# Eight matmul units of the last query step placed in other rounds of a sparse attention, and half of its compressed attention one pass later

## What is computed

```python
qg = h @ w_qg                                   # queries and gates
q = qg[..., :1024] * 64 ** -0.5
# compressed: 15 pooled keys and values for each group
s = q @ k_cmp - slope * distance
p_cmp = softmax(where(vis, s, -1e30)) * vis
o_cmp = p_cmp @ v_cmp
# selected and sliding window, each over all 256 tokens here
o_slc = softmax(q @ k_slc - slope * dist, causal) @ v_slc
o_win = softmax(q @ k_win - slope * dist, causal) @ v_win
o = gate0 * o_cmp + gate1 * o_slc + gate2 * o_win
h = h + o @ w_o
```

## Time and profile before

| | us |
|---|---|
| median of 3 runs | 971.28 |
| lowest, highest | 971.02, 973.37 |
| the profiled execution | 971.64 |
| its span, first to last instruction | 969.6 |
| PE busy in it | 953.9 (98%) |
| DVE busy | 709.0 (73%) |
| ACT busy | 488.4 (50%) |
| POOL busy | 86.9 (9%) |
| DMA read | 185.09 MB, 192 GB/s over the span |

### The profile page before, as it was taken

One profiled execution on the slowest core, in us unless ns is written; L12 is line 12 of the kernel. 1 busy time (PEld: TensorE's weight loads), 2 busy tenths in 40 slices (PEclk: granted clock), 3 DMA queues, 4 the chain that ended last, 5 costly groups with the idle time before them and its releaser, 6 DMA issues.

```text
span 969.6 us, 19370 instructions
## 1 busy us (share of the span) xinstructions
PE 953.9 (98%) x7874; PEld 920.2 (95%) x7874; DVE 709.0 (73%) x1124; ACT 488.4 (50%) x712; POOL 86.9 (9%) x132
## 2 busy tenths in 40 slices
PE   8999999999999999899999999999999999999998
PEld 8999999999999977599999999999999999999998
DVE  4986777777769878967777777688876676555654
ACT  5444634444437556847344443537667555334441
POOL 7000000000000042420100000020000000000000
PEclk9999999999999999999999999999999999999999
DMA  9856848786754762037586868435344357564621
GB/s 262 273 174 215 261 156 293 230 292 224 271 184 150 249 218 88 1 133 259 166 303 224 294 228 288 145 114 181 101 171 153 109 174 260 171 221 132 229 72 44
DMA packets 131387, 186.98 MB, mean 193 GB/s; under 512 B 6272, under 2 KB 102656, under 8 KB 131328
## 3 DMA queue, kind: packets, MB, share of 16 engines
q1 hardware_dynamic: 123984, 159.82, 50.1%
q0 software_dynamic: 6912, 25.17, 7.5%
q10 hardware_dynamic: 432, 1.16, 0.4%
HBM read 185.09 MB, written 1.05 MB: 192 GB/s over the span
## 4 chain that ended last, share of the span: by engine, by line
PE 90%; DVE 5%; ACT 2%; issue 1%; DMA 1%; POOL 0%; SPq 0%; DVEq 0%; ACTq 0%
PE ps L1886 47%; PE ps L1962 19%; PE ps L1882 12%; PE ps L1884 4%; DMA g_raw<-in_a_w_in 1%; DVE g_lo L1172 1%; PE ps L2028 1%; PE ps L2146 1%; PE ps L2161 1%; DVE e_even L1535 1%; PE ps L2081 0%; POOL bias_h L629 0%; ACT e_odd L881 0%; PE ps L2270 0%; PE ps L1944 0%
## 5 line engine op out<-in xcount | busy, mean ns | idle before, releaser
L1886 PE MATMUL ps<-opa_hi,g_hi 128*128 128x256 f32 x864 | 228.9, 286 | 1.8 <-issue 1.4
L1886 PE MATMUL ps<-opa_lo,g_hi 128*128 128x256 f32 x864 | 221.0, 283 | 0.0
L1886 PE MATMUL ps<-opa_hi,g_lo 128*128 128x256 f32 x864 | 181.5, 283 | 0.0
L1288 DVE TENSOR_TENSOR g_lo<-g_raw,g_hi 128x2048 fp32r<-128x2048 f32 x54 | 123.8, 2293 | 69.7 <-ACT g_hi L742 69.7
L1886 PEld LDWEIGHTS ps<-opa_hi,g_hi 128*128 128x128 f32 x864 | 165.7, 192 | 5.1 <-issue 4.7
L1886 PEld LDWEIGHTS ps<-opa_lo,g_hi 128*128 128x128 f32 x864 | 162.7, 192 | 0.1
L1962 PE MATMUL ps<-hid_hi,d_hi 128*128 128x256 f32 x528 | 148.0, 280 | 0.1
L1172 DVE TENSOR_TENSOR g_lo<-g_raw,g_hi 128x2048 fp32r<-128x2048 f32 x54 | 123.5, 2289 | 33.4 <-ACT g_hi L668 32.9
L1962 PE MATMUL ps<-hid_hi,d_lo 128*128 128x256 f32 x528 | 147.7, 280 | 0.0
L1962 PE MATMUL ps<-hid_lo,d_hi 128*128 128x256 f32 x528 | 147.5, 279 | 0.0
L668 ACT ACTIVATE g_hi<-g_raw 128x2048 fp32r<-128x2048 f32 x54 | 103.1, 1910 | 71.8 <-PE ps L1886 55.2
(11 more groups left out here) (337 smaller groups left out, 1809.8 us busy)
## 6 DMA issues: line engine op xcount, KB each, us to landing
g_raw<-in_f_w_gu SPq DMA_DIRECT2D x44, 1024.0 KB, 8.8
ada_raw<-in_w_ada POOLq DMA_DIRECT2D x48, 512.0 KB, 6.1
d_raw<-in_f_w_down SPq DMA_DIRECT2D x22, 1024.0 KB, 5.1
g_raw<-in_w_in SPq DMA_DIRECT2D x14, 1024.0 KB, 7.9
g_raw<-in_w_gate SPq DMA_DIRECT2D x11, 1024.0 KB, 7.2
g_raw<-in_w_up SPq DMA_DIRECT2D x11, 1024.0 KB, 9.6
d_raw<-in_w_down SPq DMA_DIRECT2D x11, 1024.0 KB, 5.2
g_raw<-in_a_w_in SPq DMA_DIRECT2D x10, 1024.0 KB, 8.2
```

Of the source, the lines that this page charges most:

```text
L1288: dve.tensor_tensor(part_view(g_lo, g0 + r, True), raw_cols(c % 2, r % 2, True), part_view(g_hi, g0 + r, True).bitcast(F32), ALU.subtract) ...
L1886: mm = pe.matmul(pair(b)[:, a, :], wt[:, a * P:(a + 1) * P], xt, **st)
```

## The change

On PE, `values(0)` moves ahead of unit 8, and the eight units of step QG + 3 go two to each of blocks 2, 3, 4 and 5, where before there were four in block 2 and four in block 3. In block 5 both stand straight behind `scores(5)`. The wait for `evac_q(3)` and `compressed_scores(1)` move from block 4 to block 5, between `turn(4, 0)` and `turn(4, 1)`. In block 6 `turn(5, 0)` goes ahead of `values(4)`. On DVE, `evac_q(3)` moves from pass 4 to pass 5, ahead of `shift(10)`, and `compressed_shift(1)` from the end of pass 4 to right behind `shift(10)`. On ACT, `compressed_exp(1)` moves from the start of pass 5 to behind its three copies, and the split of WO + 1 from the end of pass 3 to the end of pass 6. The diff is whole.

```diff
--- before.py
+++ after.py
@@ -897,8 +897,6 @@
                 act.activation(pct[:, q, :], ps[:, 6 if q else 7, 0:T], ACT.Copy).then_inc(pct_made, 1)
 
             for j in range(1, NH // 2 + 2):
-                if j == 5:
-                    compressed_exp(1)
                 if 1 < j < NH // 2:
                     exps(j, 0)
                 if j >= 2:
@@ -910,8 +908,8 @@
                         if q == 0 and j >= 2:
                             act.wait_ge(pv_done, 2 * j - 2)
                         act.activation(pt_buf[:, 512 * q:512 * q + 512], ps[:, 4 + q % 2, :], ACT.Copy).then_inc(pt_copied, 1)
-                if j == 1:
-                    compressed_exp(0)
+                if j in (1, 5):
+                    compressed_exp(j // 5)
                 if j < NH // 2:
                     exps(j, 1)
                 if j == 1:
@@ -920,7 +918,7 @@
                     split_g(WO)
                 if j == 5:
                     compressed_copy(1)
-                if j == 3:
+                if j == 6:
                     split_g(WO + 1)
             product_and_gained(WO, 3, opb_hi, opb_hi_made, "f_norm", 8)
         if last_stage >= 4:
@@ -1576,10 +1574,12 @@
                 for e in range(2):
                     if j < NH // 2 + 1:
                         normalize(2 * j - 2 + e)
-                    if j == 4 and e == 0:
+                    if j == 5 and e == 0:
                         evac_q(3)
                     if j < NH // 2:
                         shift(2 * j + e)
+                    if j == 5 and e == 0:
+                        compressed_shift(1)
                 if j == 5:
                     compressed_factors(1)
                 dve.wait_ge(opa_hi_made, 8 * A_FILL["attn"] + j - 1)
@@ -1587,8 +1587,6 @@
                                   opa_hi[:, j - 2, :].bitcast(F32), ALU.subtract).then_inc(opa_made, 1)
                 if j == 3:
                     split_g(WO)
-                if j == 4:
-                    compressed_shift(1)
                 if j == 8:
                     split_g(WO + 1)
             add_product(WO, opb_hi, opb_lo, opb_hi_made, B_FILL["n3"], opb_made, "f_norm", 8)
@@ -2184,42 +2182,46 @@
 
             scores(2)
             compressed_turn(0)
+            values(0)
             query_units(8, 1)
-            values(0)
+            turn(1, 0)
             query_units(9, 1)
-            turn(1, 0)
+            turn(1, 1)
+
+            scores(3)
             query_units(10, 1)
-            turn(1, 1)
+            values(1)
+            turn(2, 0)
             query_units(11, 1)
-
-            scores(3)
-            query_units(12, 2)
-            values(1)
-            query_units(14, 1)
-            turn(2, 0)
-            query_units(15, 1)
             turn(2, 1)
 
             pe.wait_ge(g_evac, evacs(QG + 2))
             scores(4)
             values(2)
+            query_units(12, 1)
             turn(3, 0)
+            query_units(13, 1)
+            turn(3, 1)
+
+            scores(5)
+            query_units(14, 2)
+            values(3)
+            turn(4, 0)
             pe.wait_ge(g_evac, evacs(QG + 3))
             compressed_scores(1)
-            turn(3, 1)
-
-            scores(5)
-            values(3)
-            turn(4, 0)
             turn(4, 1)
 
             for j in (5, 6):
                 scores(j + 1)
                 if j == 5:
                     compressed_turn(1)
-                values(j - 1)
-                turn(j, 0)
-                turn(j, 1)
+                    turn(j, 0)
+                    values(j - 1)
+                    turn(j, 1)
+                else:
+                    values(j - 1)
+                    turn(j, 0)
+                    turn(j, 1)
 
             out_units(0, 0, 2)
             values(6)
```

## The result

The changed kernel takes 982.89 us in the median (982.09 to 983.68, 4 runs), the kernel before 972.1 in the same comparison (971.02 to 973.37). The ratio is 1.0109, 95% interval 1.0097 to 1.0121: slower by 1.1%, 10.8 us between the two medians. The forecast was slower by 6.6 us, with a range up to 980.0. The direction is right, the size is not. The profiled execution is the shortest of the four (982.09).

What follows compares the result with a forecast made beforehand. The prediction took a ring through PE, DVE and ACT, with DVE fullest, as the bound. Moved work (-2.1), new waits and work on DVE (net 5.2) and the split (1.4) gave +6.6 us: median 977.9, range 974.8 to 980.0.

Steps and rivals of the forecast that it cites:

- the ring: Attention passes, scores(2) to first output unit: a dependency cycle through PE, DVE and ACT, 6.0 us a round; loss +6.6 us.
- All three rivals with less or no loss: Same stretch: PE's holes filled, 968.0, chance 0.04; waits hidden, 970.1, 0.10; waits or split partly hidden, 974.2 to 976.3, 0.06.
- The first of them: PE as bound: four units (3.2 us) fill its 3.98 us of idle time, less a 0.7 wait; 968.0, chance 0.04.
- the term for the clock: Behind PE's 3.1 us gap ahead of turn(4,1): clock falls to 1.2 GHz, +0.4 to +1.1 us, 978.7, chance 0.07.
- the rule: Skill statement that long PE gaps lower the clock, weighed for the 3.1 us gap: 978.7, against 977.9 by the row.
- the cover of 0.3 us: Block 6: values(4) ends at 410.9, opa_hi not before 411.16, so putting turn(5,0) first was priced at 0.
- the turned order: Block 6, turn(5,0) ahead of values(4): price 0 with cover, at most the 1.89 us of values(4) without.
- the walk: Scheduling PE, DVE and ACT by row durations through blocks 2 to 6: first output unit at 419.88 instead of 413.28.
- the sum's terms: Blocks 4 to 6: -2.1 + 2.0 + 0.72 + 2.6 + 1.25 + 0.8 is 5.3 (unrounded 5.2), plus 1.4 for the split.
- the first two terms: DVE in pass 5: 2.0 us waiting for units 14 and 15, and 0.72 for evac_q(3), both added to the loss.

Runs made afterwards that it cites:

- a2: Changed kernel with 28 unread matmuls between compressed_scores(1) and turn(4,1) only, more than that gap holds; 984.61 us, ratio 1.0123 to the kernel before.
- a3: Changed kernel with ACT's split of WO + 1 at the end of its pass 4 instead of pass 6; 979.55 us, ratio 1.0065 to the kernel before.
- a4: Changed kernel with compressed_shift(1) behind shift(11) instead of behind shift(10); 978.14 us, ratio 1.0055 to the kernel before.
- The covers: Unread matmuls put into PE's gaps in the changed kernel; with 26 of them sized to the gaps of blocks 5 and 6 and ahead of turn(6,1), 978.56 us.
- a5: Changed kernel with evac_q(3) behind shift(10) instead of ahead of it; 981.14 us, ratio 1.0099 to the kernel before.
- a8: Changed kernel with the eight units back in blocks 2 and 3 and values(0) back behind unit 8; 976.82 us, ratio 1.0050 to the kernel before.
- a6: Changed kernel with values(4) ahead of turn(5,0) again, as before the change; 980.56 us, ratio 1.0077 to the kernel before.
- b2: Changed kernel with unread matmuls in the gaps of block 6 and ahead of turn(6,1), none ahead of turn(4,1); 979.89 us, ratio 1.0085 to the kernel before.
- a1: Changed kernel with 28 unread matmuls ahead of turn(4,1), more than that gap holds, and 18 between turn(6,0) and turn(6,1); 985.06 us, ratio 1.0130.
- b1: Changed kernel with only 11 unread matmuls in the gap ahead of turn(4,1); 980.75 us, ratio 1.0094 to the kernel before.
- a7: Changed kernel with 26 unread matmuls: 11 ahead of turn(4,1), 3 ahead of compressed_turn(1), 5 ahead of turn(5,0), 7 ahead of turn(6,1); 978.56 us, ratio 1.0071.
- b3: Changed kernel with compressed_shift(1) behind shift(11), ACT's WO + 1 split in pass 4, unread matmuls in block 6 and ahead of turn(6,1); 974.17 us, ratio 1.0021.

## Why the prediction was right and wrong

**Right: the ring, wait by wait.** With the clock held, the loss is 6.44 us where 6.6 were walked. In the changed kernel itself: evac_q(3) waits 1.9 (2.0 forecast) and begins at 395.99 us (395.8), compressed_shift(1) waits 2.5 (2.6) and begins at 400.38 (400.2), turn(4,1) begins at 403.14 (403.1) behind a gap of 2.8 (3.1), exps(7,0) follows the split without idle time. Only the gap ahead of turn(5,0) is 0.84 where over 1 was forecast. The wait for `pct` in block 2 is 0.5 (0.7), and scores(3) comes 0.9 us sooner without any gain, as argued. All three rivals with less or no loss were wrong for the reason given: DVE was there first. (The first of them had a slip: 3.2 us of units can return at most 3.2, not 3.98, which makes it 968.8 and not 968.0. Nothing hangs on it.)

**Wrong: the term for the clock, in size and in chance.** The step that failed is the weighing of the rule. The prediction saw a gap that no row of before matched, priced a fall of the clock at +0.4 to +1.1 us, and gave it 0.07. It cost 3.75 in the profiled execution; the other three are longer and have a lower mean granted clock (0.991 and 0.992, against 0.993). Three things were missed. (1) The length: only turn(4,1), scores(6) and turn(5,0) were doubled, as if the clock came back with the work; it stayed low for 10 us, which took in values(4), whose end moved past ACT's arrival, so that the cover of 0.3 us named for the turned order was gone and `opa_hi` waited 1.5. The whole stretch cost 2.2 where at most 1.1 was priced. (2) The second gap: the walk itself had ACT's first copy late behind the split and PE's last transposes waiting for it until 419.46, but the clock was not asked about there; the clock fell there too, and now in the output units, where PE has no idle time to give: 3.4 us at half rate cost 1.5, close to half of them, while the 10.2 us of the first stretch cost only 2.2. (3) The chance: the rows showed no fall up to a wait of 0.84 us and nothing about 3.1, so they gave no ground for 0.93 against a fall. The traces of a2 and a3 show that even the row was weak: there the clock fell ahead of scores(2) at waits of 0.65 and less, the same that stand in the kernel before. The statement of the Trainium skill ("TensorE: Matmul & The Clock Gate", section "HAM oscillation — how this bites in real kernels"), that long gaps of PE put the clock back, agrees with the trace: 2.8 us without work, then a granted clock of 0.50. Much shorter gaps went with a fall as well (1.2 and 1.3 us in a4), which this statement doesn't cover, and there the measurement decides. With the rule taken at its word, but the price taken as before, the forecast would have been 978.7, still 4 us short; with the price that the runs show, 6.6 + 3.75 is 10.35 us, where 10.8 were measured. The other statement of the Trainium skill that was weighed ("Perfetto Trace Analysis", section "Optimization Strategies"), to keep PE as busy as possible, did not make the moved units a gain. The covers, which are work for nobody, did gain by keeping PE busy, since what counted was the clock behind a gap.

**Partly wrong: the sum's terms.** The prediction listed on DVE 2.0 for the units, 0.72 for evac_q and 2.6 for the compressed scores as things that add. a5 shows that the first two are the shadow of PE's chain: taking 1.5 us out of the wait for the units put 1.3 into the next wait. The total was right, since both lists end at the same point, but someone who had taken the first two terms for something to win would have won nothing on the ring. Moving compressed_shift(1) and the split, with the gaps covered, returns 49.15 - 45.10 = 4.05 of the 6.4; by a8 the units are 1.4. The units were moved back only with the clock free to fall, so their 1.4 is read from the start of compressed_shift(1), ahead of the fall, and the exact share of each in the 6.4 stays open.

## What to carry to other kernels

Ask of every new gap on PE not only who waits for what, but what runs behind it: a price for a gap is the gap plus what the work behind it loses at half rate until the clock is back, as far as others wait for that work, and it is dearest where PE is the bound. Where an operation is moved to the middle of another engine's pass, walk the ring of all engines once around; the idle time of an engine that isn't the ring's slowest member is no room to fill. And when a wait looks like a term, look whether the next wait on the same engine would only grow by it.

## What the runs showed of the hardware

Each trace is one execution, so what follows counts cases and is not a rule. The gap of 2.8 or 2.9 us ahead of turn(4,1) was followed by a low clock in all six traces that left it uncovered (changed, a3, a5, a6, a8, b2), for 10.2 us in three of them, 6.8 in a5 and a8, and 3.4 in b2. With that gap covered or gone, two gaps of block 6 with two transposes between them (1.2 and 1.3 us in a1, a2 and a4; 0.87 and 1.27 in b1) had a fall in or behind them in all four, for 3.4 us. In a7 and b3, where no gap of blocks 5 and 6 was over 0.63 us, it didn't fall. The gap of 2.1 ahead of the last transposes was followed by a fall in the changed kernel, a4 and a6, and by none in a5 and a8.

Shorter gaps aren't safe either. Ahead of scores(2) every kernel has waits of about 0.4 to 0.65 us in the same order of work; the clock fell there in a2 and a3 and in none of the other eleven traces. The kernel before is no exception. It ran 28 more times beside the variants: the eleven executions with a mean granted clock of 0.999 or 1.000 took 971.2 to 972.3 us, the seventeen with 0.997 or 0.998 took 972.0 to 973.9; where in the span the clock was low in these isn't known. So nearly the same order of work, and even exactly the same, can cost several us more or less; the four times of a5, two at 978.6 and two at 983.9, fit this. What decides when the clock falls and how long it stays low is open.

An unread fp32 matmul of 128 columns took two instructions of 0.11 us each, 0.23 together; 26 of them on a PE that waited anyway made the kernel 4.3 us faster.
